# Score products of the first mixer on the full height of the array

## The chip, the cores and the metric

The kernel runs on one core of one Trainium2 chip. The metric is the device time of one execution in microseconds: median 2829.69 us of three runs (2824.68 to 2833.89). The two last digits of such a number mean little; what counts is said in the prediction.

## The reference, cut to what matters

Two transformer blocks of two layers each, run one after the other on 256 tokens with width 1024. Each layer is a feed-forward part, a mixer, and a second feed-forward part. The change touches the mixer of the first block alone, which runs twice. From its projections it computes three attentions, all over head size 64, with keys and queries normalised and rotated:

```
logits = einsum('bqhd,bsd->bqhs', qi, ki)             # 8 index heads, one shared key
iscore = sum over heads of relu(logits) * wi           # then top 64 keys of each query
A: softmax(qa . ka over the selected keys) @ va        # 4 heads, one shared key
B: softmax(qb . kb, causal) @ vb                       # 4 heads, each its own key
C: (softmax(qc0 . kc0) - lam * softmax(qc1 . kc1)) @ vc   # 4 heads, two components each
merged = sigmoid(ga) * A @ wa + sigmoid(gb) * B @ wb + sigmoid(gc) * C @ wc
```

## The kernel before

One program of five engine streams, all unrolled; each engine's order of work is written out by hand, and semaphores (`up`, `at`) tie the streams together. All weights come as chunks of 2,048 columns in the order of use. SyncE loads a chunk into one of five RAW buffers when its last reader has finished (`spent`). ScalarE (ACT) rounds each half of it to its high part WHI (`hi`, line 1437), VectorE takes the low part WLO (`lo`, line 2337), and TensorE makes three fp32r products a tile: high by high, high by low, low by high. Where tokens are the rows of the result that is `tokens` (lines 388 to 390), elsewhere `pairs` (lines 377 to 379).

In the first mixer the work goes by stages j of the projection: 0 and 1 index queries, 2 the shared keys, weights and A's value, 3 A's queries, 4 and 5 B's queries and keys, 6 B's values, 7 and 9 C's queries, 8 and 10 C's keys, 11 and 12 C's values. `at_(n, j, t, p)` is one quarter of a stage: token block t of 128, half p of the depth, 12 matmuls. The result goes PSUM to STA (ACT, `tev`, line 1595), is squared for the norm (`psq`, line 1584; `pss` on VectorE, line 2552), multiplied by its gain and rotated on GpSimd (`pg`, `turn`, lines 3432 to 3447), for keys normalised on VectorE (`kn`, line 2563), transposed on TensorE into bank 7 (`ptr`, line 516) and copied by ACT to the tile QT (`qt`, lines 1619 to 1622). In QT, 128 rows hold two heads of 64: an even head on rows 0 to 63, an odd one on rows 64 to 127 (for C the two components of one head). The shared keys are doubled onto both halves.

`ix` (line 534) makes the index products in six steps, head by head with the 64 rows of that head: `re_ix` (line 1630, ACT) takes their relu, `acc` (lines 2590, 2594, VectorE) sums them, `causal` and `top` (lines 2601 to 2614) select 64 keys by eight rounds of maximum and replace, and write the selection mask SBI. `sc(n, i, x)` (lines 558 to 561) makes the scores of unit i, bank x. There are twelve units: A and B, token block 0 with four heads, token block 1 as two units of two heads; C, block 0 in two units, block 1 in four. Each head is an fp32 product on its 64 rows, for A the selection mask, and the causal mask as a bf16 product of the identity with CMB. For block 0 there are 128 keys, for block 1 there are 256. Then come `nb` (row maximum, lines 2628 and 2640, VectorE), `ex` (exponentials with row sums, line 1647, ACT), `rc` (scaling, for C also the difference, lines 2650 to 2664, VectorE), `pt` (transposes, line 574), `pe` (copy, line 1657, ACT), `pv` (value products, lines 594 and 596), `oh` or `ov` and `ol` (lines 1670, 1666, 2675). Score banks are three (0, 1, 6): a step waits until the third one before has been read. C's result is normalised (`snsq`, `sn`), transposed (`sntr`) and scaled (`snh`, `oc`). The gate projections `ag` fill TensorE from the C units on, the branch products `ab` and the output product `ao` follow. GpSimd also computes the norms of the queries (`prs`).

## Time and profile before

| | |
|---|---|
| runs, median of 3 | 2829.69 us |
| profiled execution, own time | 2827.89 us |
| its span | 2825.7 us |
| TensorE busy | 2774.2 us, 98% |
| VectorE busy | 1797.3 us, 64% |
| ScalarE busy | 1431.4 us, 51% |
| GpSimd busy | 284.8 us, 10% |
| mean granted TensorE clock | 0.992 |

The span is the time from the first to the last instruction; the own time is 2.2 us longer. PE is TensorE, DVE is VectorE, ACT is ScalarE, POOL is GpSimd. Matmuls overlap: the time of one is longer than the distance to the next, so costs are read from the distance of starts. A matmul of fp32 operands is recorded as two instructions. A wait "until issue" is one whose semaphore the profile does not name. The first mixer of the first layer (mixer 0) lies at about 215 to 450 us, that of the second layer (mixer 1) 633.8 us later.

### The profile page before, as it was taken

Reading aid. Unit: us, or ns where it says so; the run is one execution under the profiler, and the core shown is the slowest. Engines: PE = TensorE matmul, PEld = TensorE weight load, DVE = VectorE, ACT = ScalarE, POOL = GpSimd, SP = SyncE. Lnnn points to the kernel's source line nnn. Section 1 sums busy time; section 2 is a strip of 40 time slices with the busy share of each in tenths; the row PEclk is TensorE's granted clock in tenths of the full one; section 3 lists DMA queues with packets and bytes.
Section 4 is the critical chain, followed back from the end, with each engine's and each line's share of the span. In section 5 each row is a group of like instructions: output and inputs, shape, how many; then the busy total and the mean of one; then the engine's idle time right before and its main releaser. Section 6 shows DMA issues by size and latency. Waiting matters only on the chain.

```text
span 2825.7 us, 48866 instructions
## 1 busy us (share of the span) xinstructions
PE 2774.2 (98%) x20056; PEld 2571.5 (91%) x20056; DVE 1797.3 (64%) x3060; ACT 1431.4 (51%) x2435; POOL 284.8 (10%) x439
## 2 busy tenths in 40 slices
PE   9998999999999999999999999999999999999999
PEld 8997899999997899999998799999999987999998
DVE  6557757456467757456568788565565586875654
ACT  5445645444455645444446575354454465754543
POOL 0003301000003301000001312100000022111000
PEclk9999999999999999999999999999999999999999
DMA  5452244454542354554544234555454442344443
GB/s 206 191 191 105 106 178 169 181 205 164 193 180 105 113 180 161 193 193 177 189 162 164 76 134 152 186 180 186 166 193 179 170 164 77 134 163 180 164 181 147
DMA packets 64732, 462.02 MB, mean 164 GB/s; under 512 B 7296, under 2 KB 7808, under 8 KB 9344
## 3 DMA queue, kind: packets, MB, share of 16 engines
q1 hardware_dynamic: 64512, 458.90, 44.4%
q8 instruction: 160, 2.62, 0.4%
q14 instruction: 60, 0.49, 0.0%
HBM read 457.83 MB, written 1.05 MB: 162 GB/s over the span
## 4 chain that ended last, share of the span: by engine, by line
PE 84%; DVE 6%; POOL 4%; issue 4%; ACT 1%; DMA 1%; SPq 0%; DVEq 0%; POOLq 0%; ACTq 0%
PE bank L455 17%; PE bank L377 17%; PE bank L379 17%; PE bank L378 17%; PE bank L388 3%; PE bank L390 3%; PE bank L389 3%; PE bank L646 2%; DVE WLO L2337 2%; POOL MTA L3491 1%; PE bank L1085 1%; PE bank L421 1%; POOL STA L3447 1%; PE bank L1009 1%; POOL RTA L3432 1%
## 5 line engine op out<-in xcount | busy, mean ns | idle before, releaser
L2337 DVE TENSOR_TENSOR WLO<-RAW,WHI 128x1024 fp32r<-128x1024 f32 (+1 forms) x872 | 1059.8, 1254 | 299.9 <-ACT WHI L1437 299.3
L1437 ACT CAST WHI<-RAW 128x1024 fp32r<-128x1024 f32 (+1 forms) x872 | 886.1, 1047 | 392.3 <-DMA RAW<-weights_dram 222.1
L377 PE MATMUL bank<-XH,WHI 128*128 128x256 f32 x3712 | 1060.8, 286 | 3.7 <-DVE WLO L2337 3.7
L379 PE MATMUL bank<-XH,WLO 128*128 128x256 f32 x3712 | 1051.6, 283 | 0.0
L378 PE MATMUL bank<-XL,WHI 128*128 128x256 f32 x3712 | 1051.4, 283 | 0.0
L377 PEld LDWEIGHTS bank<-XH,WHI 128*128 128x128 f32 x3712 | 712.6, 192 | 11.0 <-issue 3.1
L378 PEld LDWEIGHTS bank<-XL,WHI 128*128 128x128 f32 x3712 | 712.8, 192 | 5.5
L379 PEld LDWEIGHTS bank<-XH,WLO 128*128 128x128 f32 x3712 | 712.8, 192 | 0.0
L1501 ACT ACTIVATE SG<-bank 128x256 f32<-128x256 f32 x152 | 58.7, 386 | 485.5 <-PE bank L379 485.5
L2450 DVE TENSOR_TENSOR HF<-SG,bank 128x256 f32<-128x256 f32 x152 | 63.9, 421 | 340.6 <-ACT SG L1501 340.6
L388 PE MATMUL bank<-WHI,XH 128*128 128x256 f32 (+2 forms) x928 | 271.4, 292 | 4.2 <-DVE XL L2391 4.0
L389 PE MATMUL bank<-WLO,XH 128*128 128x256 f32 (+2 forms) x928 | 264.9, 285 | 0.0
L390 PE MATMUL bank<-WHI,XL 128*128 128x256 f32 (+2 forms) x928 | 264.8, 285 | 0.0
L455 PE MATMUL bank<-WHI,HH 128*128 128x512 f32 x704 | 222.0, 396 | 0.0
L455 PE MATMUL bank<-WLO,HH 128*128 128x512 f32 x704 | 222.0, 397 | 0.0
L455 PE MATMUL bank<-WHI,HL 128*128 128x512 f32 x704 | 221.2, 395 | 0.0
L388 PEld LDWEIGHTS bank<-WHI,XH 128*128 128x128 f32 x928 | 181.0, 195 | 6.5 <-issue 5.6
L389 PEld LDWEIGHTS bank<-WLO,XH 128*128 128x128 f32 x928 | 181.2, 195 | 0.5
L390 PEld LDWEIGHTS bank<-WHI,XL 128*128 128x128 f32 x928 | 180.9, 195 | 0.0
L455 PEld LDWEIGHTS bank<-WHI,HL 128*128 128x128 f32 x704 | 133.4, 189 | 32.1
L455 PEld LDWEIGHTS bank<-WLO,HH 128*128 128x128 f32 x704 | 132.3, 188 | 32.0
L455 PEld LDWEIGHTS bank<-WHI,HH 128*128 128x128 f32 x704 | 122.7, 189 | 19.5
(339 smaller groups left out, 3186.7 us busy)
## 6 DMA issues: line engine op xcount, KB each, us to landing
RAW<-weights_dram SPq DMA_DIRECT2D x431, 1024.0 KB, 4.8
RAW<-weights_dram SPq DMA_DIRECT2D x2, 800.0 KB, 4.1
X<-x_dram SPq DMA_DIRECT2D x2, 512.0 KB, 5.6
RAW<-weights_dram SPq DMA_DIRECT2D x2, 512.0 KB, 6.6
out_dram<-X SPq DMA_DIRECT2D x2, 512.0 KB, 2.7
RAW<-weights_dram SPq DMA_DIRECT2D x2, 384.0 KB, 3.2
CM<-mixer_dram SPq DMA_DIRECT2D x2, 320.5 KB, 9.8
CM<-mixer_dram SPq DMA_DIRECT2D x2, 176.0 KB, 5.3
```

Of the source, the lines that this page charges most:

```text
L377: self.e.matmul(bank, h, xh[:, x0 + k, :], start=k == k0, stop=False)
L378: self.e.matmul(bank, h, xl[:, x0 + k, :], start=False, stop=False)
L379: ins = self.e.matmul(bank, l, xh[:, x0 + k, :], start=False, stop=k == k1)
L388: self.e.matmul(bank, xh[:, x0 + k, xs], h, start=k == k0, stop=False)
L389: self.e.matmul(bank, xh[:, x0 + k, xs], l, start=False, stop=False)
L390: ins = self.e.matmul(bank, xl[:, x0 + k, xs], h, start=False, stop=k == k1)
L455: ins = e.matmul(PS[2 * t + nh][:, :], a[:, i % HR, t * P:t * P + P], w[:, c % s, col + nh * 512:col + nh * 512 + 512], start=i == 0 and w ...
L646: ins = e.matmul(PS[2 * t + h][:, :], a[:, k, xs], w[:, c % s, i * 1024 + h * 512:i * 1024 + h * 512 + 512], start=k == 0 and w is WHI and ...
L1437: e.copy(WHI[:, c % NHI, a:b], RAW[:, c % NLO, a:b]).then_inc(*up("hi", c, p))
L1501: e.activation(SG[:, i % 2, :], PS[5 - i % 2][:, 0:256], ACT.Silu).then_inc(*up("sg", n, i))
L2337: e.tensor_tensor(WLO[:, c % NLO, a:b], RAW[:, c % NLO, a:b], WHI[:, c % NHI, a:b].bitcast(F32), ALU.subtract).then_inc(*up("lo", c, p))
L2450: e.tensor_tensor(HF[:, r, :], SG[:, r, :], PS[5 - i % 2][:, 256:512], ALU.mult).then_inc(*up("hf", n, i))
```

## The change

The fp32 products of `ix` and `sc` use all 128 rows. The stationary operand is the whole query tile with its two heads; the moving operand is a key tile in which the other head's 64 rows are zero, so that only the wanted head adds to the sum. Each key pair (stages 2, 5, 8, 10) goes to QT as two tiles, by two ACT copies of 64 partitions each. QT grows from 20 to 24 slots of 256 columns, and the tiles behind it move up by 4 KB. GpSimd zeroes slots 4 to 23 once at the start (`blank`), and in each mixer slots 0 to 3, where the index queries were, after the last index product, for the keys of stage 8. TensorE waits once for the first of these, ACT for the second in front of the copy of stage 8.

The orders of the four streams are rewritten around it. TensorE: quarter (5, 0, 1) stands in front of the first sets; (7, 0, 0), (7, 0, 1) stand behind the sets of units 2 and 5; stage 8 is no longer split by `pt` and `pv` of units 3 and 4, which move into stages 9 and 10; the transpose of stage 9 is one quarter earlier; in the C part `ag` and `sc` change places in several spots, and the first sets of unit 10 and 11 stand ahead of `sntr`. ACT: both casts of chunk 7 go behind the index relus, `ex(2)` ahead of `pe(1)`, `ex(3)` behind the evictions of stage 7. VectorE: the casts of chunks 7 to 12 go later, behind `rc(0)` to `rc(3)`; all accumulations stand in front of the first selection; `nb(9)` ahead of `sn(0)`. The diff, cut:

```diff
@@ -152,7 +152,8 @@
-QT_AT = {0: 0, 1: 2, 3: 5, 4: 8, 5: 10, 7: 12, 8: 16, 9: 14, 10: 18}
+QT_AT = {0: 0, 1: 2, 2: 4, 3: 6, 4: 10, 5: 12, 7: 16, 8: 0, 9: 18, 10: 20}
+QT_PAIR = {2: 4, 5: 2, 8: 2, 10: 2}
...
-    QT = sb("QT", [P, 20, 256], F32, at_kb(40))
+    QT = sb("QT", [P, 24, 256], F32, at_kb(40))
...
@@ Tensor.ix
-                rows = slice(64 * (h % 2), 64 * (h % 2) + 64)
-                ins = e.matmul(ps[:, i * nk:i * nk + nk], QT[rows, h // 2, t * P:t * P + P], QT[rows, 4, 0:nk], start=True, stop=True)
+                ins = e.matmul(ps[:, i * nk:i * nk + nk], QT[:, h // 2, t * P:t * P + P], QT[:, 4 + h % 2, 0:nk], start=True, stop=True)
@@ Tensor.sc
-                hf = c if m == "C" else h % 2
-                rows = slice(64 * hf, 64 * hf + 64)
-                qa = {"A": 5 + h // 2, "B": 8 + h // 2, "C": 12 + h}[m]
-                ka = {"A": 7, "B": 10 + h // 2, "C": 16 + h}[m]
-                e.matmul(ps[:, k * nk:k * nk + nk], QT[rows, qa, t * P:t * P + P], QT[rows, ka, 0:nk], start=True, stop=False)
+                qa = {"A": 6 + h // 2, "B": 10 + h // 2, "C": 16 + h}[m]
+                ka = {"A": 8 + h % 2, "B": 12 + h, "C": (0, 20)[h // 2] + 2 * (h % 2) + c}[m]
+                e.matmul(ps[:, k * nk:k * nk + nk], QT[:, qa, t * P:t * P + P], QT[:, ka, 0:nk], start=True, stop=False)
@@ Tensor.m1, in front of the first projection
             if n == 1:
...
+                self.e.wait_ge(*at("blank"))
@@ Tensor.m1, the order from stage 5 on
             self.at_(n, 5, 0, 0)
+            self.at_(n, 5, 0, 1)
             self.sc(n, 0, 0)
             self.sc(n, 0, 1)
-            self.at_(n, 5, 0, 1)
...
             self.ptr(n, 5)
-            self.at_(n, 7, 0, 0)
             self.pt(n, 0)
             self.sc(n, 1, 0)
             self.pv(n, 0)
             self.sc(n, 1, 1)
             self.sc(n, 2, 0)
-            self.at_(n, 7, 0, 1)
+            self.at_(n, 7, 0, 0)
             self.sc(n, 3, 0)
             self.pt(n, 1)
             self.sc(n, 4, 0)
+            self.sc(n, 5, 0)
             self.pv(n, 1)
+            self.at_(n, 7, 0, 1)
             self.at_(n, 7, 1, 0)
-            self.sc(n, 5, 0)
             self.pt(n, 2)
...
             self.at_(n, 10, 1, 0)
+            self.ptr(n, 9)
             self.at_(n, 10, 1, 1)
-            self.ptr(n, 9)
@@ Scalar.qt
-            if j == 2:
-                e.copy(QT[:, 4, :], PS[7][:, 0:256])
-                e.copy(QT[:, 7, :], PS[7][:, 256:512]).then_inc(*up("qt", n, j))
+            if j == 8:
+                e.wait_ge(*at("blank", n))
+            if j in QT_PAIR:
+                s, d = QT_AT[j], QT_PAIR[j]
+                ps = PS[7][:, :].rearrange("p (a q) -> p a q", q=256)
+                e.copy(QT[0:64, s:s + d + 1:d, :], ps[0:64])
+                e.copy(QT[64:P, s + 1:s + d + 2:d, :], ps[64:P]).then_inc(*up("qt", n, j))
@@ Scalar.m1
             self.tev(n, 3)
-            self.hi(c + 7, 0)
             self.re_ix(n, 0, 0)
             self.re_ix(n, 1, 0)
             self.re_ix(n, 1, 1)
-            self.hi(c + 7, 1)
...
             self.qt(n, 3)
+            self.hi(c + 7, 0)
+            self.hi(c + 7, 1)
@@ Vector.m1
             self.pss(n, 3)
-            self.lo(c + 7, 0)
             self.acc(n, 0, 0)
             self.acc(n, 1, 0)
             self.acc(n, 1, 1)
             self.acc(n, 0, 1)
+            self.acc(n, 1, 2)
             self.causal(n, 0)
-            self.acc(n, 1, 2)
+            self.acc(n, 1, 3)
             self.top(n, 0, 8, True)
-            self.acc(n, 1, 3)
...
             self.rc(n, 0)
+            self.lo(c + 7, 0)
             self.lo(c + 7, 1)
-            self.lo(c + 8, 0)
@@ Pool
+        def blank(self, n):
+            self.e.wait_ge(*at("ix", n, *M1_IX.members[-1]))
+            self.e.memset(QT[:, QT_AT[8]:QT_AT[8] + 4, :], 0.0).then_inc(*up("blank", n))
...
             self.pg(n, 3)
+            self.blank(n)
             self.prs(n, 3)
...
             self.zero()
+            self.e.memset(QT[:, 4:24, :], 0.0).then_inc(*up("blank"))
```

## Rows read from the trace of the kernel before

**Rows 1.** The page: busy time by engine, and the chain that ended last.

```profile
PE 2774.2 (98%) x20056; PEld 2571.5 (91%) x20056; DVE 1797.3 (64%) x3060; ACT 1431.4 (51%) x2435; POOL 284.8 (10%) x439
...
PE 84%; DVE 6%; POOL 4%; issue 4%; ACT 1%; DMA 1%; SPq 0%; DVEq 0%; POOLq 0%; ACTq 0%
```

**Rows 2.** Stretches of mixer 0: us, busy time (count) by engine, PEclk, DMA share, GB/s.

```profile
249.00:262.00 13.00, 10.32 (x70) 9.40 (x71) 12.07 (x41) 3.40 (x5) 3.07 (x6) 0.87 0.24 86
322.30:328.70 6.40, 6.40 (x31) 5.10 (x30) 3.55 (x11) 2.91 (x9) 0.00 (x0) 0.73 0.00 0
328.70:356.00 27.30, 26.97 (x193) 22.57 (x193) 20.83 (x58) 17.45 (x46) 0.00 (x0) 1.00 0.32 116
```

**Rows 3.** TensorE's waits, 215 to 360 us: waited for, total, times, longest.

```profile
PE bank L558 <- issue: 2.8, 1, 2.8
...
PE bank L516 <- POOL STA L3436: 2.7, 3, 1.7
...
PE bank L516 <- DVE STA L2563: 0.8, 1, 0.8
```

**Rows 4.** Matmul groups by form: the mask products, busy us, mean ns, idle.

```profile
L561 PE MATMUL bank<-CMB,IDB 128*128 128x128 bf16 x64 | 15.2, 237 | 0.0
```

**Rows 5.** TensorE in order of time, C units: start, us, engine, line, operation, count.

```profile
321.02 0.28 PE L390 MATMUL bank<-WHI,XL 128*128 128x256 f32 x1
...
321.14 0.28 PE L388 MATMUL bank<-WHI,XH 128*128 128x256 f32 x1
...
322.30 0.48 PE L558 MATMUL bank<-QT 64*128 64x128 f32 x2
...
322.88 0.48 PE L558 MATMUL bank<-QT 64*128 64x128 f32 x2
...
334.18 0.70 PE L558 MATMUL bank<-QT 64*128 64x256 f32 x2
```

**Rows 6.** TensorE in order of time, mixer 2's score sets.

```profile
1589.68 0.23 PE L1010 MATMUL bank<-CMB,IDB 128*128 128x128 bf16 x1
...
1590.11 0.48 PE L1009 MATMUL bank<-KP,QP 64*128 64x128 f32 x2
```

**Rows 7.** TensorE in order of time, the index products.

```profile
236.75 3.84 PE L534 MATMUL bank<-QT 64*128 64x128 f32 x28
241.38 1.13 PE L534 MATMUL bank<-QT 64*128 64x256 f32 x4 [0.79 <-ACT PBA L1630]
```

**Rows 8.** Stretches around the half clock; the sum is of four such stretches.

```profile
321.70:325.11 3.41, 3.41 (x21) 2.41 (x19) 1.57 (x3) 1.04 (x1) 0.00 (x0) 1.00 0.01 2
...
232.96:236.37 3.41, 1.63 (x14) 1.64 (x15) 1.64 (x3) 1.84 (x5) 1.21 (x2) 1.00 0.69 252
...
325.11:328.52 3.41, 3.41 (x16) 3.10 (x16) 2.44 (x8) 1.87 (x8) 0.00 (x0) 0.50 0.00 0
...
884.89:891.72 6.83, 6.20 (x26) 4.75 (x27) 6.34 (x21) 0.00 (x0) 0.44 (x1) 0.50 0.07 29
...
sum 17.06, PE 16.43 PEld 13.94 DVE 14.45 ACT 3.96 POOL 0.44; mean PE 4.11 PEld 3.48 DVE 3.61 ACT 0.99 POOL 0.11
```

**Rows 9.** VectorE in order of time, accumulation and key normalisation.

```profile
242.79 1.52 DVE L2594 SCALAR_TENSOR_TENSOR ISC<-PBA,SM,ISC 128x128 f32<-128x128 f32 x4 [0.22 <-ACT PBA L1630]
...
251.50 0.99 DVE L2594 SCALAR_TENSOR_TENSOR ISC<-PBA,SM,ISC 128x256 f32<-128x256 f32 x2
...
266.35 0.69 DVE L2563 TENSOR_TENSOR STA<-STA,SM 128x512 f32<-128x512 f32 x1
```

**Rows 10.** GpSimd and TensorE in order of time, stage 9.

```profile
309.84 1.32 POOL L3436 TENSOR_TENSOR STA<-RTA 128x128 f32<-128x128 f32 x1
...
311.21 0.66 PE L516 MATMUL bank<-CF,STA 128*128 128x128 f32 x4 [1.74 <-POOL STA L3436]
```

**Rows 11.** The memset's line (min/median/max ns), and ACT at the stage-10 copy.

```profile
L3420 POOL MEMSET HF<- x1: 525/525/525, 0.7 to 0.7; 128x512 f32 x1
...
320.98 0.59 ACT L1622 COPY QT<-bank 128x512 f32<-128x512 f32 x1 [1.78 <-PE bank L516]
```

More of the change, by code:

```diff
@@ L719, in m1 @@
             self.at_(n, 8, 0, 0)
+            self.at_(n, 8, 0, 1)
+            self.at_(n, 8, 1, 0)
+            self.at_(n, 8, 1, 1)
             self.pt(n, 3)
-            self.at_(n, 8, 0, 1)
-            self.pv(n, 3)
-            self.at_(n, 8, 1, 0)
-            self.pt(n, 4)
-            self.at_(n, 8, 1, 1)
-            self.pv(n, 4)
             self.ptr(n, 7)
             self.at_(n, 9, 0, 0)
-            self.pt(n, 5)
+            self.pv(n, 3)
             self.at_(n, 9, 0, 1)
-            self.pv(n, 5)
+            self.pt(n, 4)
             self.at_(n, 9, 1, 0)
+            self.pv(n, 4)
             self.at_(n, 9, 1, 1)
             self.at_(n, 10, 0, 0)
+            self.pt(n, 5)
             self.ptr(n, 8)
             self.at_(n, 10, 0, 1)
+            self.pv(n, 5)
             self.at_(n, 10, 1, 0)
+            self.ptr(n, 9)
             self.at_(n, 10, 1, 1)
-            self.ptr(n, 9)
             self.at_(n, 11, 0, 0)
@@ L751, in m1 @@
             self.at_(n, 12, 1, 1)
+            self.ag(n, 0, 0, 0)
             self.sc(n, 7, 1)
+            self.pt(n, 6)
             self.sc(n, 8, 0)
[L754 to L755 removed]
             self.pv(n, 6)
@@ L758, in m1 @@
             self.sc(n, 8, 1)
+            self.sc(n, 9, 0)
             self.pt(n, 7)
-            self.sc(n, 9, 0)
+            self.ag(n, 0, 1, 0)
             self.pv(n, 7)
-            self.ag(n, 0, 1, 0)
             self.sc(n, 9, 1)
+            self.sc(n, 10, 0)
             self.pt(n, 8)
-            self.sc(n, 10, 0)
+            self.ag(n, 0, 1, 1)
             self.pv(n, 8)
-            self.ag(n, 0, 1, 1)
+            self.sc(n, 10, 1)
+            self.sc(n, 11, 0)
+            self.ag(n, 1, 0, 0)
             self.sntr(n, 0)
-            self.ag(n, 1, 0, 0)
+            self.pt(n, 9)
             self.ag(n, 1, 0, 1)
-            self.sc(n, 10, 1)
-            self.pt(n, 9)
-            self.sc(n, 11, 0)
             self.pv(n, 9)
@@ L1751, in m1 @@
             self.ex(n, 0)
+            self.tev(n, 6)
             self.hi(c + 10, 0)
-            self.tev(n, 6)
             self.qt(n, 5)
+            self.pe(n, 0)
             self.hi(c + 10, 1)
-            self.pe(n, 0)
             self.oh(n, 0)
             self.ex(n, 1)
+            self.ex(n, 2)
             self.pe(n, 1)
-            self.ex(n, 2)
             self.oh(n, 1)
-            self.hi(c + 11, 0)
-            self.ex(n, 3)
             self.pe(n, 2)
             self.ex(n, 4)
+            self.psq(n, 7)
             self.oh(n, 2)
-            self.psq(n, 7)
             self.tev(n, 7)
+            self.ex(n, 3)
+            self.hi(c + 11, 0)
+            self.hi(c + 11, 1)
+            self.hi(c + 12, 0)
+            self.psq(n, 8)
             self.pe(n, 3)
             self.ex(n, 5)
+            self.qt(n, 7)
             self.oh(n, 3)
-            self.hi(c + 11, 1)
+            self.tev(n, 8)
+            self.hi(c + 12, 1)
             self.pe(n, 4)
-            self.hi(c + 12, 0)
-            self.psq(n, 8)
             self.oh(n, 4)
-            self.qt(n, 7)
-            self.tev(n, 8)
-            self.pe(n, 5)
-            self.hi(c + 12, 1)
-            self.oh(n, 5)
             self.hi(c + 13, 0)
@@ L1784, in m1 @@
             self.tev(n, 9)
+            self.pe(n, 5)
+            self.qt(n, 8)
+            self.oh(n, 5)
             self.hi(c + 13, 1)
-            self.qt(n, 8)
+            self.qt(n, 9)
             self.hi(c + 14, 0)
             self.psq(n, 10)
-            self.qt(n, 9)
             self.tev(n, 10)
@@ L1808, in m1 @@
             self.pe(n, 8)
+            self.ex(n, 9)
+            self.gtt(n, 0)
             self.oh(n, 8)
-            self.gtt(n, 0)
-            self.snh(n, 0)
-            self.ex(n, 9)
             self.hi(c + 17, 1)
             self.pe(n, 9)
+            self.snh(n, 0)
             self.ex(n, 10)
@@ L2774, in m1 @@
             self.lo(c + 10, 0)
-            self.rc(n, 3)
-            self.lo(c + 10, 1)
-            self.ol(n, 2)
             self.rc(n, 4)
             self.nb(n, 5)
+            self.ol(n, 2)
             self.pss(n, 7)
+            self.lo(c + 10, 1)
+            self.rc(n, 3)
+            self.lo(c + 11, 0)
+            self.lo(c + 11, 1)
+            self.lo(c + 12, 0)
             self.rc(n, 5)
             self.ol(n, 3)
-            self.lo(c + 11, 0)
-            self.lo(c + 11, 1)
+            self.pss(n, 8)
+            self.kn(n, 8)
             self.ol(n, 4)
-            self.pss(n, 8)
-            self.lo(c + 12, 0)
-            self.kn(n, 8)
-            self.ol(n, 5)
             self.pss(n, 9)
@@ L2792, in m1 @@
             self.lo(c + 13, 0)
+            self.ol(n, 5)
             self.lo(c + 13, 1)
@@ L2814, in m1 @@
             self.lo(c + 17, 1)
+            self.oc(n, 0)
             self.rc(n, 10)
```

34 lines of the change are left out of this document (16 added, 18 removed).

## The prediction

> **What bounds the kernel now.** I read the page first: TensorE is busy 98% of the span and holds 84% of the chain that ended last [rows 1]. Over the whole kernel, then, microseconds come from TensorE's own work or its few waits. The change touches only the two first-block mixers, so I next read stretches of the first one (mixer 0, about 215 to 360 us; mixer 1 repeats it 633.8 us later). There VectorE is nearly as full as TensorE: 12.07 of 13.00 us from 249 to 262, 20.83 of 27.30 us from 328.7 to 356 [rows 2]. TensorE's waits in mixer 0 are short: 2.8 us in front of the first score set (for the top-k selection on VectorE), 2.7 us at transposes waiting for GpSimd, 0.8 us for VectorE's key normalisation [rows 3]. So a saving on TensorE counts only where the softmax and selection chain keeps up.
>
> A "set" below is one head's scores for one query block: an fp32 product, seen as two matmul records of 64 rows, and a bf16 mask product on 128 rows. There are 64 sets [rows 4], 32 a mixer, half of them 128 and half 256 keys wide. A "quarter" is 12 projection matmuls (four k-tiles, one token block); their records follow one another by 0.12 us [rows 5], 1.43 us a quarter.
>
> **The set.** Sets of 128 keys start 0.58 us apart (322.30, 322.88); one of 256 has a pair 0.22 us longer, so about 0.79 [rows 5]. In mixer 2 the array goes from the same mask to a full-height fp32 pair and then to a 64-row pair: mask at 1589.68, 64-row product after the pair at 1590.11 [rows 6]. Mask plus full-height pair is thus 0.43 us, including the hand-over to 64 rows. The 28 index records in a row need 3.84 us, 0.14 us each, with no mask between [rows 7]: neighbours of one height run dense, and the gap belongs to the change of height. It is passed twice a set, and 0.58 less the columns of a dense set (below) leaves 0.29, some 0.1 where the array is handed over and the rest a weight load that nothing covers. Bounds for a new 128-key set: 0.43 us above (the hand-over stays), 0.29 below (two records at 0.11, half of the 0.21 that the 256-wide index records keep, and 0.07 for the mask). I take 0.34, 0.43 less the 0.10 that a change of height adds on one side, nearest to rows 6, where mask and pair are exactly those of the change. Saving: 0.24 a set (0.15 to 0.29), 7.7 us a mixer (4.8 to 9.3), 15.4 in all before waits.
>
> **The index products.** 32 records a mixer. Today 28 take 3.84 us and the last four, 256 wide, 1.13, of which the last record's own run-out is a fifth [rows 7]. At 0.11 for 16 narrow and 0.21 for 16 wide records, one after another would be 5.2 us against 4.4 from start to start now: the even and odd heads, on different array halves, overlap, and the change gives that up. It loses 0.8 us a mixer on TensorE. But TensorE already waits 0.79 us there for an eviction held back by VectorE's accumulation, so I charge nothing; without that cover it is 0.8. The Trainium skill, "TensorE: Matmul & The Clock Gate", Part 3, says products of small contraction in different row groups run concurrently, which speaks against this change. The trace agrees for the index products, and by the rule alone the sum would be 1.6 us worse; the score sets gain nothing from it, as a full-height mask stands between any two.
>
> **The clock.** From 321.70 to 325.11 TensorE is busy throughout, mostly with 64-row sets, and the next 3.41 us are granted 0.50 of the clock (1.2 instead of 2.4 GHz). From 232.96 to 236.37 it is busy only 1.63 us, with full-height work, and no drop follows. Four stretches at 0.50 sum to 17.06 us in the two mixers [rows 8]. Such a stretch advances the work of 1.7 us; as part of a set is not array time, I count 1.4 us lost in each. Dense full-height sets should remove the one after the C sets, in both mixers. The other, after the first sets, follows an idle wait as well; I don't count on losing it.
>
> **First half, by the new order.** (a) Selection. Taking the weight cast for chunk 7 out of VectorE's way starts accumulation about 0.4 us sooner and, with the ACT cast gone as well, gains 0.6 by 242.79. But the last accumulation (0.99 us) now precedes the first top-k [rows 9]. The first set can start at 252.2 instead of 251.68. TensorE fills with one more quarter (1.43), so its wait is 2.3, not 2.8. (b) From there to the transpose of stage 5, TensorE needs 14.6 us now; less that quarter, four sets (1.0) and perhaps the drop (1.5), it needs 10.7 to 12.2. The transpose waits for VectorE's normalisation, ending at 267.04 [rows 9]. VectorE runs from 251.5 to there without idling and does nothing TensorE could shorten; it gains 0.4. TensorE so waits 2.2 to 3.7 us where it waited 0.8, and all but 0.4 us of the saving so far is given back. (c) Then sets, transposes and value products of units 1 to 5 with three projection quarters moved behind them. Going item by item through the new order (row maximum 0.43 or 0.69 us, normaliser 0.27, exponentials 1.85 or 1.1, reciprocal and scaling 0.75 to 1.6, eviction 0.6, cast 1.2), TensorE waits about 0.6 for the now later normalised probabilities and 0.3 for the query-key copy, and comes out of unit 2's value product at 284.4 instead of 286.2. (d) Up to stage 9's transpose one quarter less lies ahead than before. GpSimd's rotary step decides there: its wait is 1.7 of the 2.7 us [rows 3], and each of its small operations takes 1.3 us while VectorE casts [rows 10]. Stage 9 reaches it 3.4 us sooner, so the transpose starts at 307.4 against 311.21; less the quarter, 2.4 us are gained. The long idle in (b) may bring a new stretch at half clock around 267 to 270, some 0.5 us on average: **1.9 us** for the half, bounds 0 and 4.
>
> **Second half.** 16 sets save 3.8 us and the drop 1.4: 5.2. VectorE was busy 3.55 of 6.40 and 20.83 of 27.30 us [rows 2], 24.4 in all; the same work must fit in 28.5 us. Walking units 6 to 11, I find new waits of 0.2 to 0.7 us at six places (transposes for the scaled probabilities, sets for a bank the exponentials have not left), 1.9 net of the old 0.3. That leaves **3.5 us**, bounds 1 and 5.2.
>
> **Small parts.** Query-key copies for stages 2, 5, 8, 10 become two ACT copies on 64 partitions. I give each the full 0.59 us of a 128x512 copy [rows 11], as an upper end: at most 2.2 us more of ACT a mixer. ACT idles 1.78 us before the stage-10 copy, and the first C sets wait for a quarter anyway; only stage 5's is on the path (the 0.3 above). If the cover were gone, 0.5 us each. The memset of 1,024 columns a mixer is 1.05 us by the 0.525 for 512 [rows 11]; it runs on GpSimd ahead of the stage-3 norms, which VectorE wants only after both top-k selections, many microseconds later. The 5,120-column one at the start is 5.3 us, while GpSimd has nothing else and the input is still being loaded and normalised: nothing, at most 0.5 if VectorE's first small operations wait for it. No DMA changes; the casts of chunks 7 to 12 on ACT and VectorE are later by up to 5 us, and the queue's refills with them, against quarters that are later too: nothing, at worst 1 us. The added waits on the memsets are long satisfied.
>
> **Sum.** 2 x (1.9 + 3.5) = 10.8, plus 0.3 because mixer 1's first drop is 6.83 us long [rows 8] and one half of it should go: 11.1 us. The profiled execution took 2827.89, which gives 2816.8; the median of the runs is 1.8 higher, so **2818.6 us**, 0.4% faster. What a measurement of this kernel can tell from no change is about 0.3%, 8.5 us.
>
> **Rivals.** Nothing new waits: 15.4 for the sets, 2.8 for the C drops, 1.5 or so for the selection wait: 2810. Against it stands (b), where the trace shows VectorE without an idle microsecond. 0.12.
> The chain takes the second half too: VectorE, 86% busy there (24.4 of 28.5), leaves 1 us of each 5.2, and the total is 2 x 2.9 = 5.8: 2824. For it: VectorE's share; against: casts may slide behind. 0.24.
> The change does not do what it says: the mask's weight load after fp32 still costs the hand-over, 0.43 a set. Then 16 x 0.09 = 1.4 less in each second half, and the clock may drop again (1.4): 5.5 less, 2824. Rows 6 speak against half of it. 0.07.
> Slower: three quarters that stood between sets and transposes are moved behind, and casts are queued in twos and threes ahead of the row maxima. If each of 12 units a mixer then waits one more cast of 1.2 us on VectorE, that is 14.4 against 7.7 + 1.4 saved, 5.3 a mixer worse: 2840. It decides from 0.8 us a unit. My walk finds 0.2 to 0.3. 0.07.
>
> **Chances.** The forecast case (8.5 to 15 us) has 0.50; with the first rival 0.62 for faster; 0.31 within 0.3%; 0.07 slower. The range 2809 to 2827 takes in the bounds of both halves and the "same" cases and leaves out about 2 in 10.
>
> **What would show it.** After: sets of 128 keys 0.34 us apart in the C units, 256 about 0.55; no 0.50 clock after them; index products about 5 us; a wait of 2 to 4 us before stage 5's transpose for VectorE; the first set near 252 us; stage 9's transpose near 307.5; unit 10's value product near 346 (351.8 now). The forecast fails if sets stay over 0.45 us apart, if the waits in the C units pass 3 us, or if the clock drops for long after the idle in (b).

## The result and the profile after

| | before | changed |
|---|---|---|
| median of 6 runs each, same chip | 2831.36 us | 2817.19 us (2814.54 to 2818.61) |
| ratio, 95% interval | | 0.9949 (0.994 to 0.9959) |
| profiled execution, own time | 2827.89 | 2815.74 |
| its span | 2825.7 | 2813.8 |

The kernel is 0.5% faster, more than the 0.3% that a measurement can tell, and 1.4 us from the forecast of 2818.6. The profiled executions differ by 12.2 us, the medians by 14.2.

The page of the changed kernel, busy time and chain (before: [rows 1]):

```profile
PE 2762.2 (98%) x20056; PEld 2572.7 (91%) x20056; DVE 1791.9 (64%) x3060; ACT 1433.7 (51%) x2441; POOL 283.7 (10%) x442
PE 86%; DVE 8%; ACT 2%; POOL 2%; issue 1%; DMA 1%; SPq 0%; DVEq 0%; POOLq 0%; ACTq 0%
```

TensorE lost 12.0 us of busy time with the same number of instructions, and VectorE's share of the chain rose from 6% to 8%: the saving is array time, and part of it ran into VectorE.

TensorE in order of time, changed kernel (start, us, engine, line, operation, count; before: [rows 5, 7]). The first two C sets, two 256-key sets, the index products, unit 10's value product:

```profile
319.57 0.49 PE L556 MATMUL bank<-QT 128*128 128x128 f32 x2
319.89 0.22 PE L559 MATMUL bank<-CMB,IDB 128*128 128x128 bf16 x1
319.95 0.44 PE L556 MATMUL bank<-QT 128*128 128x128 f32 x2
320.23 0.22 PE L559 MATMUL bank<-CMB,IDB 128*128 128x128 bf16 x1
320.28 0.44 PE L556 MATMUL bank<-QT 128*128 128x128 f32 x2
...
328.40 0.70 PE L556 MATMUL bank<-QT 128*128 128x256 f32 x2
328.94 0.22 PE L559 MATMUL bank<-CMB,IDB 128*128 128x128 bf16 x1
328.99 0.65 PE L556 MATMUL bank<-QT 128*128 128x256 f32 x2
...
237.53 5.48 PE L534 MATMUL bank<-QT 128*128 128x128 f32 x32
...
345.04 0.61 PE L594 MATMUL bank<-VT,PTA 128*128 128x128 f32 x4
```

Sets of 128 keys are now 0.33 to 0.38 us apart (0.58 before), sets of 256 keys 0.59.

TensorE's waits, 215 to 360 us (waited for, total, times, longest; before: [rows 3]):

```profile
PE bank L517 <- DVE STA L2566: 2.9, 1, 2.9
PE bank L517 <- ACT STA L1612: 2.0, 1, 2.0
PE bank L556 <- issue: 1.7, 1, 1.7
PE bank L517 <- POOL STA L3444: 0.9, 2, 0.5
PE bank L572 <- DVE PBA L2667: 0.6, 2, 0.3
PE bank L572 <- DVE PBA L2658: 0.3, 1, 0.3
PE bank L556 <- ACT QT L1623: 0.3, 1, 0.3
PE bank L556 <- ACT PBA L1650: 0.3, 1, 0.3
```

The wait before stage 5's transpose (L2566 is VectorE's key normalisation) grew from 0.8 to 2.9 us; the 1.7 us that stage 9 waited for GpSimd is gone. The 2.0 us for ScalarE, before stage 2's transpose, and 0.9 to 1.0 us for GpSimd in two short waits stood in the kernel before as well; the rest is 0.3 us each.

Stretches of mixer 0 and, the last two, of mixer 1, changed kernel (stretch, length, busy time and count of PE, PEld, DVE, ACT, POOL, then PEclk, DMA share, GB/s; before: [rows 2, 8]):

```profile
249.00:262.00 13.00, 11.27 (x98) 11.05 (x97) 12.07 (x43) 4.78 (x7) 5.82 (x12) 1.00 0.39 153
234.30:237.70 3.40, 3.40 (x17) 3.40 (x17) 0.86 (x2) 2.03 (x4) 0.63 (x1) 0.50 0.57 236
265.00:268.40 3.40, 1.72 (x12) 1.23 (x12) 3.30 (x10) 3.20 (x7) 1.23 (x4) 1.00 0.68 282
268.40:271.80 3.40, 3.40 (x20) 2.64 (x19) 1.29 (x3) 1.47 (x3) 0.00 (x0) 0.50 0.00 0
319.57:326.00 6.43, 6.30 (x54) 5.97 (x53) 5.12 (x13) 4.42 (x12) 0.00 (x0) 1.00 0.26 73
326.00:349.30 23.30, 22.73 (x173) 20.33 (x172) 19.43 (x56) 15.94 (x44) 0.00 (x0) 1.00 0.31 116
...
862.32:865.73 3.41, 3.41 (x19) 3.41 (x18) 0.80 (x2) 1.75 (x3) 1.31 (x2) 0.50 0.49 204
893.04:899.87 6.83, 5.92 (x28) 4.41 (x29) 4.26 (x9) 4.25 (x7) 0.91 (x2) 0.50 0.24 102
```

No drop of the clock follows the C sets any more. But the two first mixers together have 17.06 us at half clock in both kernels: all four drops of the kernel before went, and in mixer 0 one at 234.3 (behind the 1.97 us wait for ScalarE) and one at 268.4 (behind the wait before stage 5) came, in mixer 1 the last two rows above, at the same two waits. The wait for ScalarE alone doesn't bring the first: the kernel before has it too, and no drop there [rows 8].

Where the gain arises: at the first C set the changed kernel is 2.73 us ahead (319.57 against 322.30), at the last value product of mixer 0 6.77, after mixer 1 12.55. 0.54 us of it was there before mixer 0 began.

### The profile page after: what moved, and what is told of

Read it like the earlier page. It is cut to its first block, busy times and chain, and to the rows that moved or that the text cites. A ratio compares the mean times of both kernels' runs of the same rounds, so it can differ in the third digit from the quotient of the medians.

```text
span 2813.8 us, 48877 instructions
## 1 busy us (share of the span) xinstructions
PE 2762.2 (98%) x20056; PEld 2572.7 (91%) x20056; DVE 1791.9 (64%) x3060; ACT 1433.7 (51%) x2441; POOL 283.7 (10%) x442
## 4 chain that ended last, share of the span: by engine, by line
PE 86%; DVE 8%; ACT 2%; POOL 2%; issue 1%; DMA 1%; SPq 0%; DVEq 0%; POOLq 0%; ACTq 0%
PE bank L456 17%; PE bank L378 17%; PE bank L380 17%; PE bank L379 17%; PE bank L389 3%; PE bank L391 3%; PE bank L390 3%; PE bank L644 2%; DVE WLO L2340 2%; POOL MTA L3499 1%; PE bank L1084 1%; PE bank L422 1%; DMA RAW<-weights_dram 1%; ACT PBA L1650 1%; PE bank L1008 1%
```

## The experiments

Three questions: is it the change of height that costs, or the 64 rows; how much of the gain belongs to the new order of the work; and is it VectorE that holds back the first half. Two kernels leave work out, x4_no_mask and z2_short_top. In all kernels the lines outside the quoted edit are those of the kernel named. Ratios are to the kernel before, timed on the same chip in the same session.

| run | runs | ratio (95%) | median us |
|---|---|---|---|
| x1_old_order | 12 | 0.9979 (0.997 to 0.9989) | 2824.04 |
| x2_half_rows | 12 | 1.0002 (0.9991 to 1.0013) | 2833.72 |
| x3_c_only | 11 | 0.9988 (0.998 to 0.9997) | 2828.28 |
| x4_no_mask | 1 | no interval | 2824.32 |
| y2_half_grouped | 11 | 0.9975 (0.9967 to 0.9984) | 2824.45 |
| z1_c_half | 10 | 0.9981 (0.9971 to 0.999) | 2824.83 |
| z2_short_top | 4 | 0.9905 (0.9891 to 0.9918) | 2803.33 |
| w1_spread | 5 | 0.9941 (0.9928 to 0.9953) | 2815.89 |
| y1_rope_grouped | 5 | 0.9925 (0.9913 to 0.9937) | 2809.86 |
| w2_both | 5 | 0.9914 (0.9901 to 0.9928) | 2808.13 |

### The change of height by itself

**x4_no_mask**: the kernel before, the first mixers' score products without both masks. It was run once, so its trace counts and not its time.

```diff
-                e.matmul(ps[:, k * nk:k * nk + nk], QT[rows, qa, t * P:t * P + P], QT[rows, ka, 0:nk], start=True, stop=False)
-                if m == "A":
-                    e.matmul(ps[:, k * nk:k * nk + nk], IDB[:, :], SBI[:, t, 0:nk], start=False, stop=False)
-                ins = e.matmul(ps[:, k * nk + t * P:k * nk + t * P + P], IDB[:, :], CMB[:, :], start=False, stop=True)
+                ins = e.matmul(ps[:, k * nk:k * nk + nk], QT[rows, qa, t * P:t * P + P], QT[rows, ka, 0:nk], start=True, stop=True)
```

> The kernel before without the causal and selection mask products in the scores of the first mixer (they are left out). It asks whether a set is long because the array changes height. My theory: the 64-row products then run as densely as the index products, six C sets of 128 keys in 1.4 us or less (0.22 each, less where neighbours use different halves) in place of 3.45. Rival, a 64-row fp32 product is slow by itself: 0.40 or more each, 2.4 us for six.

TensorE in order of time, six C sets:

```profile
321.98 0.28 PE L390 MATMUL bank<-WHI,XL 128*128 128x256 f32 x1
322.19 1.16 PE L558 MATMUL bank<-QT 64*128 64x128 f32 x12
323.27 0.39 PE L388 MATMUL bank<-WHI,XH 128*128 128x256 f32 x1
```

The twelve 64-row records take 1.08 us, 0.09 each, where six sets took 3.5 before. Six bf16 masks cannot be the 2.4 us between: in the changed kernel six sets take 2.0 us with their masks. Part of the 0.09 is overlap: record by record in the trace, the first eight, four on each half, start in pairs, the later pairs 0.11 us apart; the last four lie on one half and start 0.11 us apart, each by itself. That is still no more than a full-height record takes between its like (0.11 in y1_rope_grouped, below). So a 64-row product is cheap between its like; what costs is the change of height on both sides. Of the 0.24 us between the old set and the new one, each of the two changes has 0.12.

By the Trainium skill, "TensorEngine Tiling (Array Packing)", Tiling Modes, a change of tiling mode drains TensorE. The runs agree with a cost at each change, and put its size at 0.12 us here.

**y2_half_grouped** tests this in the whole kernel: x2_half_rows (below) with the products of a bank sorted by height.

```diff
-                e.matmul(ps[:, k * nk:k * nk + nk], QT[rows, qa, t * P:t * P + P], QT[rows, ka, 0:nk], start=True, stop=False)
-                if m == "A":
+                e.matmul(ps[:, k * nk:k * nk + nk], QT[rows, qa, t * P:t * P + P], QT[rows, ka, 0:nk], start=k == 0, stop=False)
+            if m == "A":
+                for k in range(len(groups[x])):
                     e.matmul(ps[:, k * nk:k * nk + nk], IDB[:, :], SBI[:, t, 0:nk], start=False, stop=False)
-                ins = e.matmul(ps[:, k * nk + t * P:k * nk + t * P + P], IDB[:, :], CMB[:, :], start=False, stop=True)
+            for k in range(len(groups[x])):
+                ins = e.matmul(ps[:, k * nk + t * P:k * nk + t * P + P], IDB[:, :], CMB[:, :], start=False, stop=k == len(groups[x]) - 1)
```

> The kernel of x2_half_rows (the changed kernel's order, all index and score products of the first mixer on 64 rows) with one edit: in a bank the two key products stand together, then the selection masks, then the causal masks, so that the height changes twice a bank instead of twice a set. Nothing is left out. THEORY height change alone: of some 128 changes in 64 sets half go, 0.12 us each, and in the C banks the two key products lie on different halves and overlap: 8 to 10 us below x2_half_rows, 2824 to 2826 us. THEORY clock: with 64-row products about TensorE's clock stays at half for 10 to 24 us of the first half as in x2_half_rows, and most of the saving there is hidden behind the same stretch or changed little: 2828 to 2832. The profile's granted clock in the first half tells them apart.

It is 9.3 us below x2_half_rows by the medians, 7.6 by the ratios (0.0027 of 2831): the first theory's size, but not all of it is the first theory's cause. The expectation counted too much: in a C bank both products lie on the same half, and C's eight sets of 256 keys stand alone in their banks, so 24 of 64 changes a mixer go, not half, some 6 us for both mixers at 0.12 each. The clock has a part as well. The twelve runs of x2 have a mean granted clock of 0.985 to 0.991, the eleven of y2 0.989 to 0.991, and the long stretches of the second theory are in y2's trace too (below). At the same clock of 0.991, x2's one run took 2825.8 us and y2's five 2821.5 to 2823.8: 2 to 4 us, with only one run on the side of x2. The C units alone, from first set to last value product, take 29.98 us in y2 and 31.16 in x2 where no drop of the clock falls into them, 1.2 us less a mixer.

Sorting needs no tiles of zeros (y2 still makes them; a kernel without was not run), and it reaches about half of what full height reaches in the same order (16.5 and 15.0).

### Order, height, and where the height is

**x1_old_order**: full-height products, zero tiles and split copies, but the orders of work of the kernel before on TensorE, ScalarE and VectorE (long lists of calls; the first lines of the edit on TensorE).

```diff
             self.at_(n, 5, 0, 0)
-            self.at_(n, 5, 0, 1)
             self.sc(n, 0, 0)
             self.sc(n, 0, 1)
+            self.at_(n, 5, 0, 1)
             self.at_(n, 5, 1, 0)
```

> Full-height products with the copies and memsets of the change, but the four streams in the order of before. My theory: sets come 0.34 us apart, index products take about 5 us, the clock does not drop after the C sets; in the first half TensorE is held by VectorE at stage 5's transpose all the same, and some savings turn into waits between sets: 8 to 10 us faster than before (ratio 0.9965 to 0.9972). Rival 1, the order only tidies up: as the changed kernel, 14 us faster (0.995). Rival 2, the order does most of it: within 4 us of before.

**x2_half_rows**: the changed order and tiles, but index and score products on 64 rows (the same edit in `ix` is not shown).

```diff
+                hf = c if m == "C" else h % 2
+                rows = slice(64 * hf, 64 * hf + 64)
-                e.matmul(..., QT[:, qa, t * P:t * P + P], QT[:, ka, 0:nk], start=True, stop=False)
+                e.matmul(..., QT[rows, qa, t * P:t * P + P], QT[rows, ka, 0:nk], start=True, stop=False)
```

> The changed kernel (its order, tiles, copies and memsets) with all index and score products back on the 64 rows of their head. My theory: sets are 0.58 us apart, the C sets are followed by a half clock again, and the order alone brings within 3 us of before (ratio 0.999 to 1.001). Rival, the order does most of it: 6 us or more faster (0.998 or less). Rival, the new order needs the short sets: 4 us or more slower than before (1.0015 or more).

**x3_c_only**: x2_half_rows with full height in the C units alone.

```diff
-                rows = slice(64 * hf, 64 * hf + 64)
+                rows = slice(64 * hf, 64 * hf + 64) if m != "C" else slice(0, P)
```

> The changed kernel with full height in the C units alone; index products and units A and B are on 64 rows. My theory: the C part saves 4 us a mixer, and the A and B sets lie in the part that VectorE holds, where part of their saving is lost: 9 to 11 us faster than before, so 3 to 5 us of the 14 belong to A, B and index products. Rival, nothing is worth anything in front of VectorE's chain: as the changed kernel within 1 us. Rival, a saved set counts in full everywhere: 16 sets at 0.24 a mixer less, 7.7 us slower than the changed kernel.

**z1_c_half**: the complement; the index products are full height too.

```diff
-                e.matmul(ps[:, k * nk:k * nk + nk], QT[:, qa, t * P:t * P + P], QT[:, ka, 0:nk], start=True, stop=False)
+                hf = c if m == "C" else h % 2
+                rows = slice(64 * hf, 64 * hf + 64) if m == "C" else slice(0, P)
+                e.matmul(ps[:, k * nk:k * nk + nk], QT[rows, qa, t * P:t * P + P], QT[rows, ka, 0:nk], start=True, stop=False)
```

> The changed kernel with only the C units' 32 key products put back on 64 rows (QT's tiles as changed, half of them read); A, B and the index products stay full height. The complement of x3_c_only, which gained 5.4 us on x2_half_rows. THEORY heights and clock: the A and B sets keep the clock at full, so the first half is as in the changed kernel (stage 5 to stage 7 transposes 25.7 us apart, half-clock stretches of 3.41 us only), the C sets cost 32 x 0.24 = 7.7 us less what hides, and the half-clock stretch after the six C sets comes back (1.4 a mixer): 2822 to 2826 us. THEORY any 64-row product holds the clock down: long half-clock stretches (over 6.83 us) appear in the C half and the time is 2828 or more.

By the ratios (0.001 is 2.8 us, and about the half-width of each interval) the order alone gives nothing (1.0002), height in the old order 5.9 us, both together 14.4. Piece by piece in the new order: the C units' height is worth 4.0 us (x2 to x3) or 9.0 (z1 to the changed kernel), that of index, A and B 5.9 (x2 to z1) or 11.0 (x3 to the changed kernel); by the medians 5.4, 7.6, 8.9 and 11.1. x3's expectation of 9 to 11 us failed. x1 fell below its 8 to 10, though its interval (to 0.997, 8.5 us) still touches them. The order alone carries nothing, C height alone 3.4 us, and the half with A, B and the index products comes out 2 us above the C units, which these intervals do not separate.

In the C units the trace splits the gain. From first set to last value product they take 33.4 and 33.0 us in the two mixers before, 30.4 and 30.5 with full height in the old order (x1), 31.2 with 64 rows in the new order and no drop of the clock (x2b below, both mixers), and 29.3 with both.

The clock shows one reason. The schedule from stage 5's to stage 7's transposes, in x2_half_rows:

```profile
267.60:271.20 3.60, 2.57 (x16) 1.72 (x18) 3.18 (x8) 3.56 (x6) 3.23 (x4) 1.00 0.74 269
271.20:295.10 23.90, 23.90 (x88) 15.63 (x89) 11.45 (x24) 4.63 (x16) 0.88 (x4) 0.50 0.01 4
295.10:304.70 9.60, 9.60 (x81) 9.29 (x81) 6.87 (x15) 7.33 (x16) 5.05 (x6) 1.00 0.33 110
```

and in x3_c_only and y2_half_grouped (second mixer):

```profile
272.00:292.48 20.48, 20.48 (x74) 13.30 (x73) 10.75 (x23) 4.03 (x14) 0.00 (x0) 0.50 0.00 1
900.00:920.48 20.48, 20.48 (x82) 14.65 (x82) 10.25 (x23) 5.23 (x16) 0.00 (x0) 0.50 0.00 1
```

and in z1_c_half, where A and B are full height, this stretch and the one after the C sets:

```profile
274.10:293.92 19.82, 19.56 (x153) 17.54 (x153) 17.61 (x37) 11.23 (x30) 5.02 (x6) 1.00 0.15 54
321.90:325.30 3.40, 3.40 (x19) 2.34 (x20) 2.11 (x5) 1.40 (x3) 0.00 (x0) 1.00 0.00 0
325.30:328.70 3.40, 3.40 (x18) 3.40 (x18) 2.46 (x8) 2.26 (x10) 0.00 (x0) 0.50 0.02 5
```

TensorE is busy for all 23.90 us at 0.50, with 64-row sets among the work. With the C sets on 64 rows the drop after them is back, in both mixers of z1. But 64 rows don't always bring it: of the twelve mixers profiled with 64-row C sets seven have it (both of the kernel before, of z1 and of x4, the first of x2) and five do not (the second of x2, both of x2b and of y2), while none of the sixteen with full-height ones has it.

The granted clock, averaged over all runs of a kernel, points the way of the long stretches: 0.991 for the kernel before and 0.992 for the changed one, but 0.988 for x2 and 0.989 for x3. To see whether the long stretches belong to the kernel or to one execution, two kernels were profiled again.

**x2b_half_rows**, the same as x2_half_rows:

> x2_half_rows again, one more profiled execution. The first had 58 us at half clock in the two first mixers, 23.9 of them from 271.2 on, where the changed kernel had 17.1 in all and the kernel before 17.1. THEORY 64-row products in the changed order keep the clock at half: again at least one stretch of 10 us or more in the A and B units and over 30 us in the two mixers. THEORY draw: no stretch over 6.83 us there and about 17 to 20 us in the two mixers.

**x1b_old_order**, the same as x1_old_order:

> x1_old_order again, one more profiled execution, because the first was its slowest of twelve (2833.57 against a median of 2824.04) with a stretch of 20.48 us at half clock in the second mixer, where nothing was changed. THEORY draw: that stretch belongs to the one execution; here the time is 2821 to 2827 us and no stretch at half clock is over 6.83 us. THEORY the kernel: a stretch of 10 us or more stands there again, near 1580.

x2b took 2828.56 us and has two stretches of 10.24 us at half clock, in the same place of each mixer, and 30.7 in both: shorter than the first time, still as the first theory said. Between the same two transposes it needed 30.62 us with 10.24 at half clock, x2 37.09 with 23.89 (start to start in the trace): 0.47 us lost for each us at half clock. x1b took 2833.21 us and its stretch in mixer 2, where nothing was changed, came again:

```profile
1581.00:1601.00 20.00, 20.00 (x78) 16.16 (x78) 8.67 (x19) 5.91 (x15) 1.04 (x1) 0.51 0.08 31
```

So it was no draw of one execution: both profiled executions of this kernel have it. But it does not stand for the kernel either. Its eleven other runs are 4 us or more below these two, and their mean granted clock is 0.990 to 0.995 against 0.988. What brings the stretch, so far from the edit, is not shown. One profile can sit at the slow end of a kernel's runs. The stretch covers mixer 2's score sets, which have 64-row rope products.

### VectorE's chain

**z2_short_top**: half of the selection's rounds left out.

```diff
-            self.top(n, 0, 8, True)
+            self.top(n, 0, 4, True)
             self.causal(n, 1)
-            self.top(n, 1, 8, True)
+            self.top(n, 1, 4, True)
```

> The changed kernel with 4 instead of 8 rounds of the selection of each row of keys in the first mixer (half of the selection is left out), which takes about 2.9 and 3.9 us of VectorE a mixer from the chain ahead of the stage-5 transpose. THEORY VectorE's chain bounds the first half: the idle time of 1.73 us before the first A set and of 2.88 before the stage-5 transpose goes, with the small waits of 0.3: 4.5 to 6 us a mixer, 2806 to 2809 us. THEORY another chain (ScalarE's copies or the weights) stands right behind: the wait before the stage-5 transpose stays over 1.5 us and the gain is under 4 us (2813 or more).

Its waits of TensorE, 249 to 296 us, all:

```profile
PE bank L556 <- ACT QT L1623: 0.7, 1, 0.7
PE bank L517 <- DVE STA L2566: 0.4, 1, 0.4
PE bank L572 <- DVE PBA L2658: 0.4, 1, 0.4
PE bank L556 <- ACT PBA L1650: 0.3, 1, 0.3
```

It is 13.9 us below the changed kernel by the medians, 12.5 by the ratios, more than expected: the 1.7 us are gone and 0.4 is left of the 2.9, and with them the drops of the clock behind them (one of 3.41 us is left in both mixers). From stage 0's transposes to the first C set the trace is 6.9 us shorter in mixer 0 and 6.2 in mixer 1, so the gain lies where it was looked for. The time belongs to a kernel that selects fewer keys.

**w1_spread** keeps the work and moves it.

```diff
-            self.acc(n, 1, 3)
             self.top(n, 0, 8, True)
+            self.acc(n, 1, 3)
             self.causal(n, 1)
-            self.top(n, 1, 8, True)
+            self.top(n, 1, 1, False)
             self.pss(n, 4)
-            self.pss(n, 5)
             self.nb(n, 0)
+            self.top(n, 1, 2, False)
+            self.pss(n, 5)
             self.kn(n, 5)
+            self.top(n, 1, 1, False)
             self.rc(n, 0)
+            self.top(n, 1, 4, True)
```

> The changed kernel with VectorE's order in the first half of the first mixer rearranged, nothing left out and nothing added: the last index head is accumulated behind the first selection (1.0 us earlier for the first A sets), and the squares' sums, the first unit's maxima and the key normalization of stage 5 stand between rounds of the second selection, whose result the third unit needs only some 11 us after it is ready now. THEORY VectorE's chain alone bounds these places (as the shortened selection says): the idle time of 1.73 before the first A set falls to 0.7, that of 2.88 before the stage-5 transpose goes, 3 to 4 us a mixer, 2809 to 2812 us. THEORY the work only moves: VectorE is busy 12 us out of 13 here, so what is put behind (second selection, low parts of weights c+7) makes the third unit's sets or the token products wait about as much: new idle of 2 us or more between the stage-5 and stage-7 transposes, 2815 to 2819 us.

TensorE's waits in it after 250 us, in order of time:

```profile
252.92 0.46 PE L556 MATMUL bank<-QT 128*128 128x128 f32 x2 [0.83 <-issue]
265.56 0.66 PE L572 MATMUL bank<-CF,PBA 128*128 128x128 f32 x4 [1.35 <-DVE PBA L2658]
266.45 0.49 PE L556 MATMUL bank<-QT 128*128 128x128 f32 x2 [0.23 <-ACT QT L1623]
274.90 0.45 PE L556 MATMUL bank<-QT 128*128 128x256 f32 x1 [1.59 <-ACT PBA L1650]
```

The wait before stage 5 is gone and that of the first set halved, but 1.35 and 1.59 us stand at the next places. Counted from stage 0's transposes, stage 5's come 3.8 us sooner than in the changed kernel (37.6 us against 41.4) and stage 7's only 1.0 (66.1 against 67.1). By the medians it is 1.3 us faster, by the ratios 2.3, which the intervals do not separate from nothing: most of the waiting only moved. Less work on VectorE took it away, this other order did not.

### The same cure in the other mixers

**y1_rope_grouped**: the changed kernel, the score products of the two mixers of the second kind sorted by height within a bank.

```diff
             for k, h in enumerate(hs):
-                rows = slice(64 * (h % 2), 64 * (h % 2) + 64)
-                o = ps[:, k * nk:k * nk + nk]
-                e.matmul(o, QN[:, h, qs], KN[:, h, 0:nk], start=True, stop=False)
-                e.matmul(o, QP[rows, h // 2, qs], KP[rows, h // 2, 0:nk], start=False, stop=False)
-                ins = e.matmul(ps[:, k * nk + t * P:k * nk + t * P + P], IDB[:, :], CMB[:, :], start=False, stop=True)
+                e.matmul(ps[:, k * nk:k * nk + nk], QN[:, h, qs], KN[:, h, 0:nk], start=k == 0, stop=False)
+            for k, h in enumerate(hs):
+                rows = slice(64 * (h % 2), 64 * (h % 2) + 64)
+                e.matmul(ps[:, k * nk:k * nk + nk], QP[rows, h // 2, qs], KP[rows, h // 2, 0:nk], start=False, stop=False)
+            for k, h in enumerate(hs):
+                ins = e.matmul(ps[:, k * nk + t * P:k * nk + t * P + P], IDB[:, :], CMB[:, :], start=False, stop=k == len(hs) - 1)
```

> The changed kernel with one edit in the two mixers of the second kind: a bank's score products are issued by height, first all keys of 128 rows, then all rope keys of 64 rows, then all mask products, so the height changes twice a bank instead of twice a set (12 banks with 32 sets over the two mixers... per mixer 2 banks of 4 sets and 4 banks of 2). Nothing is left out. In the changed kernel the 128-key sets of these mixers start 0.85 us apart and the 256-key sets 1.22. THEORY height change: what a 64-row product costs is the change of height before and behind it, some 0.12 to 0.15 us each: of 64 changes a mixer pair 128-key banks save 4 x 6 = 24 and 256-key banks 8 x 2 = 16, 40 changes in all, 5 to 6 us: 2811 to 2813 us, and the sets' bank of four takes 2.5 us instead of 3.4. THEORY half rows: a 64-row product is dear by itself wherever it stands: within 1 us of the changed kernel (2816 to 2818).

Two sets in the changed kernel, then a bank of four 128-key sets in y1_rope_grouped and the start of the next:

```profile
1576.26 0.49 PE L1008 MATMUL bank<-KP,QP 64*128 64x128 f32 x2
1576.68 0.23 PE L1009 MATMUL bank<-CMB,IDB 128*128 128x128 bf16 x1
1576.74 0.44 PE L1007 MATMUL bank<-KN,QN 128*128 128x128 f32 x2
1577.11 0.48 PE L1008 MATMUL bank<-KP,QP 64*128 64x128 f32 x2
...
1572.83 1.05 PE L1005 MATMUL bank<-KN,QN 128*128 128x128 f32 x8
1573.81 1.16 PE L1008 MATMUL bank<-KP,QP 64*128 64x128 f32 x8
1574.90 0.40 PE L1010 MATMUL bank<-CMB,IDB 128*128 128x128 bf16 x4
1575.13 1.11 PE L1005 MATMUL bank<-KN,QN 128*128 128x128 f32 x8
```

A bank takes 2.30 us instead of 3.4, and the kernel is 7.3 us faster than the changed one by the medians (6.8 by the ratios), a little more than the 5 to 6 expected. The score products themselves account for it: summed from start to start over both mixers they take 34.2 us in the changed kernel's trace and 26.7 here. Eight 64-row records cost 1.09 us, eight full-height ones 0.98 to 1.04; within a run both start 0.11 us apart, and the two records at a change of height 0.20 and 0.21. The half-empty product is not dear, the change next to it is.

**w2_both**, the edits of w1_spread and y1_rope_grouped together:

> w1_spread and y1_rope_grouped together: the changed kernel with VectorE's order rearranged in the first mixer and the score products of the second mixer grouped by height. They touch different stretches. THEORY the two gains add: y1 gave 7.3 us, w1 3 to 4 a mixer, so 2802 to 2804 us, below both kernels and below y1_rope_grouped. THEORY the rearrangement gives nothing: as y1_rope_grouped, 2809 to 2811 us.

2808.13 us, 0.9914: the fastest kernel that computes everything, 23 us below the kernel before, though its interval overlaps y1's. The 2802 to 2804 us of the first theory failed; only y1's part is shown to count.

## Why the prediction was right, point by point

**The set.** 0.34 us for 128 keys was forecast, 0.33 to 0.38 measured, and x4, y1 and y2 show the reason given, the hand-over between heights. For 256 keys 0.55 was forecast and 0.59 measured. The term "16 sets save 3.8 us" was too large: summing the distances between starts by kind, sets and masks of mixer 0's C units take 10.6 us before and 7.5 after, 3.0 saved (2.7 in mixer 1, where less of the drop falls on the sets). The 0.24 was carried from the 128-key set to the wide one, which saves 0.2.

**The waits of the second half.** 1.9 us net was charged for six new waits; TensorE idles 0.70 us where it idled 0.33. This miss of 1.5 us and the last one of 0.8 go opposite ways: the second half gains 4.0 us in mixer 0 and 3.7 in mixer 1, against 3.5.

**The clock.** The drop after the C sets went in both mixers, and came back in z1 with the 64-row C sets. z1's C units take 32.65 us from first set to last value product, x2b's, also on 64 rows and in the same order but without the drop, 31.16; x2 has both values, one in each mixer. The drop is worth 1.5 us, forecast 1.4. The reason given, that 64-row sets bring it, is half shown: full-height sets never had it behind them, but 64-row ones were without it in five of twelve mixers. What the forecast put down as "some 0.5 us on average" for a new drop near 267 to 270 was a full one, at 268.4, in this execution, and the drop at 234.3 was not forecast. From stage 2's transposes to the first index product it is 3.39 us now (234.14 to 237.53) and was 2.01. VectorE's accumulation, with which the long chain begins, so starts at 239.33, 0.4 later than before, where the forecast had it 0.4 sooner. Against these two stands the drop after the first sets, which the forecast did not count on losing and which went. The sum at half clock stayed 17.06 us; the 0.3 that the sum took for mixer 1 was not there, as a stretch of 6.83 us stands there again, at 893.0.

**The index products.** 5.31 us to the start of stage 3's transpose (237.53 to 242.84), forecast 5.2; the old wait of 0.79 among them is gone. The 4.4 us that the forecast set against it are too few: without that wait, the old ones took 4.9 us from their start to stage 3's transpose (236.75 to 242.44, less 0.79), so the lost overlap is 0.4 us and not 0.8. It costs nothing here: stage 3's transpose is 0.4 us later while the first set still waits 1.7 us for VectorE's selection, and VectorE does not wait once for index scores after 239.33. As for the overlap itself, x4's pairs on two halves, 0.11 us apart, against single full-height records 0.11 us apart in y1 agree with the rule of the Trainium skill, "TensorE: Matmul & The Clock Gate", Part 3, cited in the prediction.

**First half.** The first set at 252.36 (forecast 252.2); the wait before it 1.73 (2.3), shorter since TensorE arrived later; before stage 5 2.88 us (2.2 to 3.7), and z2 shows that VectorE's amount of work is behind both. The next step, (c), missed: TensorE comes out of unit 2's value product at 285.47, where 284.4 was forecast and 286.23 measured before, 0.8 us gained instead of 1.8. The drop at 268.4, which lies in this stretch and which the forecast priced apart at 0.5, is about the size of the miss. Stage 9's transpose stands at 307.20 all the same (307.4), and that agreement is luck. GpSimd was to hold TensorE there for 1.3 us or so (284.4 plus the 21.7 us of work in between is 306.1); TensorE came 1.1 us later than that and did not wait. GpSimd was ready by then, because two of its four small steps took 0.32 and 0.46 us rather than 1.3; at 1.3 each it would have held the transpose to about 308.8. Net of the 0.54 us of head start the half gains 2.2 us, in mixer 1 2.1, against 1.9.

**Sum.** 12.0 us in the profiled executions, net of the head start, against 11.1 forecast, 12.55 with it. The two copies, the memsets and the queue show in no wait except the 0.3 us for the query-key copy, which was forecast. So the mechanisms of the forecast hold (the set, the drop after the C sets, the wait for VectorE), and the closeness of the total is partly luck: a saving of the sets too large by 0.8 us against waits too large by 1.5, one drop not foreseen against one not counted on, a late value product against an early GpSimd.

**The rivals.** "Nothing new waits" fell with the 2.88 us. "The chain takes the second half too" fell with 0.70 us of idle time there. "The mask's weight load still costs the hand-over" fell with the sets. "Slower" needed 0.8 us a unit; the new waits are 0.3. What no case had was that the new order is worth something only with the full height: alone it measures 1.0002, with it 0.0030 of the time (x1 to the changed kernel), 8.5 us.

## What to carry to other kernels

Where a 64-row fp32 product stood next to a 128-row product, TensorE lost 0.12 us or somewhat more at each change; look at the distance between starts and compare it with a run of the same form. Before buying full height with tiles of zeros and memory, sort the products of a bank by height: one start at the first, one stop at the last. Where a bank holds one set alone, as in C's wide units, there is nothing to sort. And where a faster engine runs into another's chain, halve that chain's work for one run before rearranging it: z2 showed a bound, and w1 that the one reordering tried mostly moved the waiting elsewhere.

## What was unexpected in the hardware

Once at half clock, TensorE stayed there in several profiles for 10.24 to 23.9 us though it was busy 96 to 100% of the time (two exceptions below). In the changed order with 64-row A and B sets (x2, x2b, x3, y2) such a stretch stands behind stage 5's transposes in all eight mixers profiled; with full-height ones (changed kernel, y1, z1, z2, w1, w2) none of the twelve has one over 6.83 us, and none of the four of x1 and x1b in the old order. It is not the 64 rows alone: the kernel before has them too and no stretch over 6.83, and z1 (from 1557.5 us) and w2 (from 2316.3) have one of 10.24 us ahead of any 64-row product of that mixer, there with 1.4 us of idle time in it. The length changes from one execution to the next (23.9 and 10.24 us at the same place in x2 and x2b). What brings such a stretch and what lets it end was not isolated.
